# A hybrid decoder step: states, convolution rows, norm weights and sub keys laid out with channels or state dimension on the partitions

## The chip, the cores and the metric

One core of a Trainium2 chip. The metric is the time of one execution in device microseconds, as the median of several runs. All data are float32.

## What is computed

One step of a two-layer decoder trunk for 256 prompt tokens and 64 sample tokens (8 sequences of 8). Layer 0 is a Mamba-2 mixer, a PEER mixer and a per-layer embedding; layer 1 is dilated attention over a shared K/V, a PEER mixer and an embedding. The change touches the Mamba mixer of layer 0 and PEER's sub keys:

```python
def mamba_mixer(u, conv_buf, h0, w_in, conv_w, conv_b, dt_bias, a_log, d_skip, norm_g, w_out):
    zxbcdt = u @ w_in                                   # z 2048, xBC 4096, dt 32 columns
    xbc, new_buf = causal_conv(xbc, conv_buf, conv_w, conv_b)   # 4 taps, the last 3 rows are kept
    xbc = silu(xbc)                                     # xs 2048 (32 heads of 64), B and C 8 groups of 128
    dt = softplus(dt + dt_bias); a = -exp(a_log)
    y, h = ssd_scan(xs, dt, a, bm, cm, h0)
    y = (y + d_skip * xs) * silu(z)
    y = group_rmsnorm(y) * norm_g                       # 8 groups of 256
    return y @ w_out, new_buf, h
# in ssd_scan, per chunk and group of 4 heads (state h: 64 x 128 per head)
    y = ((C B^T) * decay) @ (xs dt) + (C h) * exp(cum)
    h = h * exp(cum[-1]) + B^T (tail * xs dt)
# in peer: scores of the queries against sub_keys (2 x 128 keys of 128)
```

The prompt starts from zero states; each sample sequence starts from its own state and convolution rows. New convolution rows and final states are outputs. Each PEER mixer picks 128 experts a token, gathers 4 KB rows of two tables for them, and sums.

## The kernel before

The program is written engine by engine, with explicit semaphores; TensorE writes into 8 PSUM banks used in turn (`claim` waits until the bank's last user is done, `freeing` marks that). Up to the first gather it goes through these stages:

1. `norm`, `dt`, then z (`gate_block`, L598): four blocks of 512 columns over all 320 tokens. Between the first and the second block PE transposes the 29 convolution rows (24 state rows, 4 taps, 1 bias) and the norm's weights (L625 to L629); ACT copies them to `stT` and `ngT` (L1467).
2. The xBC projection (L641), 32 channel blocks with channels on the partitions, each with POOL's copies of state rows (L2543 to L2546), ACT's eviction, DVE's convolution and silu; `to_tokens` turns the results back. Then PE turns the new convolution rows (L652), ACT copies them (L1500), SP stores them in 16 pieces (L1279, L1280).
3. `cum` and `ec`: cumulated decays, and the whole decay of each sample sequence and head (L804 to L813).
4. The scan: 24 steps, 8 groups for each of two prompt tiles of 128 tokens and for the sample tile (t = 2). In a step PE makes the decay and C B^T products of the next step (`scan_front`), then y and the state update (`scan_back`); DVE masks, adds and gates; POOL scales by dt and decays (L2550 to L2589); ACT takes exponentials and squares. The prompt's final states are turned by PE (`final_state`, L700), copied by ACT (L1568) and stored per group.
5. In a sample step two blocks of state (two heads, 8 sequences) are in turn: SP loads a block as (head, channel) x sequence x state dimension (L1295), PE turns 16 pieces of 128x128 (`sample_turn`, L657), ACT copies them to `h0T` (L1558), PE reads the states with C (L675) and makes the update (L683), POOL scales the unturned state (L2589), DVE adds the update into `hnew` (L2138), SP stores it (L1286). Beside these steps run the prompt tile's output products (`out_block`, L779), PEER's queries (L762) and scores (L747), and from group 3 on DVE's picks of experts (L2063 and on).
6. POOL starts the gathers (L2610) when the scan is over (L2202), the last states are stored and the first experts are chosen. From there a written order of phases interleaves gathers, dot products on DVE (L2255), sums on PE (L1129) and the rest of the network; SP streams the weights.

SP issues all other transfers in one fixed order and waits in that order; weights go through a ring of four 1 MB slots.

## Time and profile before

| | |
|---|---|
| median of 3 runs | 2504.68 us (2501.03 to 2508.19) |
| the profiled execution | 2497.27 us |
| its span, first to last instruction | 2495.5 us |
| PE busy | 1745.5 us (70%) |
| DVE busy | 1569.1 us (63%) |
| POOL busy | 1339.7 us (54%) |
| ACT busy | 305.7 us (12%) |
| read from HBM, written | 845.26 MB, 12.17 MB |

The span is the time inside the core; the execution's own time has about 2 us around it. PE's busy time is of pipelined products and says little of how near its peak it is; the shares are means over stages that have different limits. The profile attributes idle time of an engine to what ended it; of an engine that isn't the limit of its stage it costs nothing.

### The profile page before, as it was taken

The page shows a single profiled execution, that of the slowest core. Times are in us where ns is not written, and L with a number is a line of the kernel's source. Part 1 is how long each engine was busy: PE and PEld are TensorE (multiplying, and loading weights), DVE is VectorE, ACT ScalarE, POOL GpSimd, SP SyncE. Part 2 cuts the span into 40 slices and gives each one's busy share as a digit, 9 for nine tenths or more (in the row PEclk, how much of TensorE's full clock was granted, in tenths as well). Part 3 has the DMA queues.
Part 4 walks back from the last instruction along what each step waited for, and adds up shares of the span by engine and source line. Part 5 has one row for each costly group of instructions (what it writes and reads, how often), then busy time and mean ns, then how long its engine had stood idle before and what let it go on. Part 6 is the DMA issues. An engine that isn't in the chain of part 4 may idle for free.

```text
span 2495.5 us, 23767 instructions
## 1 busy us (share of the span) xinstructions
PE 1745.5 (70%) x7752; PEld 786.5 (32%) x7752; DVE 1569.1 (63%) x3811; ACT 305.7 (12%) x709; POOL 1339.7 (54%) x1496
## 2 busy tenths in 40 slices
PE   7999789594406666678787767776745758556678
PEld 4577758433400010022334224341213422001112
DVE  2488767999798657652635989768754543833321
ACT  2133313101000000001101012110012200000000
POOL 0011634266547777755674456655454643577774
PEclk9999899796756677789799787887878969699999
DMA  4331256499979999999999999999999989999997
GB/s 158 129 108 68 94 173 231 136 398 416 417 265 413 420 420 420 420 411 416 400 418 416 416 416 372 418 415 415 415 385 365 349 318 365 388 419 420 419 419 308
DMA packets 325848, 859.14 MB, mean 344 GB/s; under 512 B 26841, under 2 KB 93353, under 8 KB 325697
## 3 DMA queue, kind: packets, MB, share of 16 engines
q0 software_dynamic: 184320, 671.17, 66.5%
q1 hardware_dynamic: 141406, 186.46, 20.9%
q8 instruction: 62, 1.02, 0.2%
q14 instruction: 60, 0.49, 0.1%
HBM read 845.26 MB, written 12.17 MB: 344 GB/s over the span
## 4 chain that ended last, share of the span: by engine, by line
POOL 21%; DMA 17%; PE 12%; issue 9%; DVE 8%; SPq 4%; ACT 0%; POOLq 0%; DVEq 0%; ACTq 0%
POOL arena L2610 21%; DMA arena<-peer_v,arena 7%; PE banks L922 4%; DMA wring<-w_q 4%; PE banks L1129 3%; DVE arena L2255 3%; DMA wring<-cache_v 2%; SPq L1365 2%; PE banks L1038 1%; SPq L1363 1%; DMA wring<-peer_w_query 1%; DMA wring<-w_kv 1%; PE banks L860 1%; PE banks L565 1%; DMA arena<-peer_u,arena 1%
## 5 line engine op out<-in xcount | busy, mean ns | idle before, releaser
L2255 DVE SCALAR_TENSOR_TENSOR arena<-arena,banks 128x1024 f32<-128x1024 f32 x640 | 762.0, 1219 | 408.0 <-DMA arena<-peer_u,arena 401.9
L1129 PE MATMUL banks<-arena 128*32 128x512 f32 x2560 | 678.8, 714 | 334.8 <-DMA arena<-peer_v,arena 328.3
L2610 POOL DMA_INDIRECT arena<-peer_v,arena x640 | 608.3, 951 | 401.1 <-issue 202.2
L2610 POOL DMA_INDIRECT arena<-peer_u,arena x640 | 605.3, 946 | 380.6 <-issue 189.7
L1129 PEld LDWEIGHTS banks<-arena 128*32 128x32 f32 x2560 | 91.1, 116 | 795.8 <-DMA arena<-peer_v,arena 630.6
L922 PE MATMUL banks<-wring,uT 128*128 128x512 f32 (+3 forms) x448 | 223.3, 648 | 59.6 <-DMA wring<-w_q 26.5
L565 PE MATMUL banks<-cst,arena 128*128 128x128 f32 (+6 forms) x498 | 75.6, 299 | 161.5 <-DVE arena L2271 82.5
L922 PEld LDWEIGHTS banks<-wring,uT 128*128 128x128 f32 (+1 forms) x448 | 80.1, 189 | 209.1 <-issue 164.7
L646 PE MATMUL banks<-uT,wring 128*128 128x320 f32 x512 | 139.1, 433 | 0.0
L565 PEld LDWEIGHTS banks<-cst,arena 128*128 128x128 f32 (+6 forms) x498 | 58.9, 153 | 212.1 <-DVE arena L2271 82.7
L646 PEld LDWEIGHTS banks<-uT,wring 128*128 128x128 f32 x512 | 96.7, 190 | 39.8 <-issue 0.4
L2545 POOL COPY arena<-arena 128x3 f32<-128x3 f32 x32 | 6.0, 187 | 176.2 <-ACT arena L1491 176.2
L565 PE MATMUL banks<-cst,u 128*128 128x128 f32 (+1 forms) x256 | 43.3, 332 | 74.0 <-DVE u L1936 62.9
L860 PE MATMUL banks<-uT,wring 128*128 128x128 f32 x512 | 69.5, 294 | 9.6 <-issue 9.6
L860 PEld LDWEIGHTS banks<-uT,wring 128*128 128x128 f32 x512 | 64.2, 205 | 34.0 <-issue 34.0
L609 PE MATMUL banks<-wring,uT 128*128 128x512 f32 (+1 forms) x256 | 73.2, 499 | 0.0
L2063 DVE MAX8 arena<-arena 128x8 f32<-128x128 f32 (+1 forms) x208 | 60.6, 333 | 19.1 <-ACT arena L1528 18.2
L2066 DVE FIND_INDEX8 arena<-arena 128x8 uint32<-128x128 f32 (+1 forms) x208 | 67.3, 336 | 0.0
L565 PEld LDWEIGHTS banks<-cst,u 128*128 128x128 f32 (+1 forms) x256 | 35.6, 180 | 99.8 <-DVE u L1936 58.7
L1157 PE MATMUL banks<-wring,uT 128*64 128x512 f32 (+1 forms) x128 | 59.1, 614 | 3.4 <-DVE uT L2038 3.4
L2306 DVE TENSOR_SCALAR arena<-arena 128x512 f32<-128x512 f32 (+1 forms) x10 | 4.4, 441 | 86.8 <-ACT arena L1666 86.6
L1038 PE MATMUL banks<-wring,arena 128*64 128x128 f32 x208 | 28.0, 299 | 41.6 <-DMA wring<-cache_v 40.2
(271 smaller groups left out, 1971.9 us busy)
## 6 DMA issues: line engine op xcount, KB each, us to landing
wring<-peer_w_query SPq DMA_DIRECT2D x40, 1024.0 KB, 18.6
wring<-ssm_w_in SPq DMA_DIRECT2D x24, 1024.0 KB, 7.3
wring<-w_q SPq DMA_DIRECT2D x18, 1024.0 KB, 22.7
wring<-ssm_w_out SPq DMA_DIRECT2D x16, 1024.0 KB, 8.6
wring<-ple_w_gate SPq DMA_DIRECT2D x12, 1024.0 KB, 11.8
arena<-peer_u,arena POOLq DMA_INDIRECT x640, 10.0
arena<-peer_v,arena POOLq DMA_INDIRECT x640, 8.9
out_sample_ssm<-arena SPq DMA_DIRECT2D x16, 512.0 KB, 5.6
```

What stands on the lines that cost most here:

```text
L565: mm = pe.transpose(bank[0:c, col:col + r], src, ident[0:r, 0:r])
L609: mm = pe.matmul(out, uT[:, kk, OFF[t]:OFF[t] + ROWS[t]], cols, start=(kk == 0), stop=(kk == KD - 1))
L646: mm = pe.matmul(acc[:, 0:NTOK], w[k // 4][:, k % 4, j * 128:(j + 1) * 128], uT[:, k, :], start=(k == 0), stop=(k == KD - 1))
L860: mm = pe.matmul(bank[:, 0:R], w[k // 4][:, k % 4, (b % 4) * 128:(b % 4 + 1) * 128], uT[:, k, OFF[t]:OFF[t] + R], start=(k == 0), stop=(k ...
L922: mm = pe.matmul(bank[0:ROWS[t], 0:w.shape[2]], uT[:, kk, OFF[t]:OFF[t] + ROWS[t]], w[:, k, :], start=(kk == 0), stop=(kk == kchunks - 1))
L1038: pe.matmul(bank[rows, 0:128], pts[:, b, rows], cache[:, 1, 13 * b2 + b, :], start=(b == 0), stop=False)
L1129: mm = pe.matmul(sums(t, at, half), place_of(t, at), rows_buf[:, k, half * 512:(half + 1) * 512], start=at < spots(t), stop=False, skip_gr ...
L1157: mm = pe.matmul(acc[t][0:ROWS[t], :], uT[:, kk, OFF[t]:OFF[t] + ROWS[t]], w[:, k, :], start=(kk == 0), stop=(kk == 15))
L2063: step(j, dve.max(out_v[:, o], values))
L2066: step(j, dve.max_index(out_i[:, o], out_v[:, o], values))
L2255: dve.scalar_tensor_tensor(rows_buf[:, k, :], rows_buf[:, k, :], 1.0, u_now, ALU.mult, ALU.mult, accum_out=pact[:, n % 2, at:at + 1]).then ...
L2610: pool.indirect_dma_start(rows_buf[:, k, :], None, tables[kind], bass.IndirectOffsetOnAxis(ap=rows, axis=0))\
```

## The change

Inputs and outputs are laid out on the host so that the state dimension or the channels come first: convolution rows (128 x 32 x 29), the norm's weights (128 x 16), sub keys (128 x 2 x 128 a layer), sample states (8 groups x 128 x 8 sequences x 256), prompt states (128 x 8 x 256), new convolution rows (128 x 32 x 27). On the chip the transposes and copies that made these layouts go. A block of sample state is now one group of four heads for four sequences. POOL scales it out of its load buffer into `hnew` and so waits for that buffer's last store; DVE adds the update in place; the update has the sequence's B rows as weights and its x rows moving. The decay of each sequence and head comes from one product with a block-masked `da` that DVE writes. DVE waits for the store of the new convolution rows before it clears the scan's area.

```diff
-            pe.wait_ge(rows_in.sem, 64)
-            for half in range(2):
-                transposes(("rows", half), [(j * 29, conv_rows[:, (16 * half + j) * 128:(16 * half + j + 1) * 128])
-                                            for j in range(16)])
-            transposes("ng", [(0, ng_rows)])
...
-            for q in range(8):
-                for j in range(4):
-                    pe.wait_ge(*pool_done.at(("newrow", 4 * q + j)))
-                transposes(("newst", q), [(j * 128, newT[:, 4 * q + j, :]) for j in range(4)])
...
-                for i in range(2):
-                    for q in range(2):
-                        pe.wait_ge(*freed(("h0T", 2 * g + i, q)))
+                for q in range(2):
+                    pe.wait_ge(*h0_in[(2 * g + q) % 4].at(2 * g + q))
                 bank = claim(pe, ("inter", 2, g))
                 for b in range(8):
                     for i in range(2):
-                        mm = pe.matmul(bank[64 * i:64 * i + 64, 0:128], ctm[:, g % 2, b, :], h0T[:, i, b, :],
+                        mm = pe.matmul(bank[64 * i:64 * i + 64, 0:128], ctm[:, g % 2, b, :],
+                                       h0[(2 * g + b // 4) % 4][:, b % 4, 128 * i:128 * i + 128],
                                        start=(b == 0), stop=(b == 7))
...
+                acc = {(q, c): claim(pe, ("hupd", 2 * g + q, c)) for q in range(2) for c in range(2)}
+                for b in range(2):
                     for q in range(2):
-                        rows = slice(64 * i + 32 * q, 64 * i + 32 * q + 32)
-                        bank = claim(pe, ("hupd", 2 * g + i, q))
-                        mm = pe.matmul(bank[:, :], xdtt[rows, x, i * 128:(i + 1) * 128],
-                                       bm[rows, g % 2, :, :], start=True, stop=True)
-                        mm.then_inc(*full(("hupd", 2 * g + i, q)))
+                        for c in range(2):
+                            rows = slice(64 * c + 32 * q, 64 * c + 32 * q + 32)
+                            mm = pe.matmul(acc[q, c][:, 256 * b:256 * b + 256], bm[rows, g % 2, 2 * c + b, :], xdtt[rows, x, :],
+                                           start=True, stop=True)
...
             bank = claim(pe, "ec")
-            for hd in range(HEADS):
-                rows, k = slice(64 * (hd % 2), 64 * (hd % 2) + 64), hd // 2
-                mm = pe.matmul(bank[rows, k * 8:(k + 1) * 8], da[0:64, 2, hd:hd + 1].to_broadcast([64, 64]),
-                               cst[0:64, C_BM:C_BM + 8], start=True, stop=True)
-            mm.then_inc(*full("ec"))
+            pe.matmul(bank[:, 0:256], ones[0:64, :], da_of, start=True, stop=True).then_inc(*full("ec"))
...
+            sp.wait_ge(*pool_done.at(("newrow", CONV_BLKS - 1)))
+            sp.dma_start(O["new_conv"], newT).then_inc(*newst_out.mark("all", 16))
...
                 if blk >= 4:
-                    sp.wait_ge(*dve_done.at(("hnew", blk - 4)))
...
+                    sp.wait_ge(*pool_done.at(("h0s", blk - 4)))
+                    sp.wait_ge(*full_at(("inter", 2, blk // 2 - 2)))
...
-            for g in range(6):
-                store_final(g)
+            store_final(0)
             sp.wait_ge(*full_at(("state", 1, 7)))
             load_state(2)
             load_state(3)
+            store_final(1)
             load_weights(sp, load_index[("out", 0, 0)] + 8)
-            for g in (6, 7):
-                store_final(g)
...
                 if t == 0:
-                    sp.dma_start(sk_raw, I["peer_sub_keys"][1].rearrange("c k d -> k c d")).then_inc(*sk_in.mark(1, 16))
+                    sp.wait_ge(*full_at(("score", 0, 2, 1)))
+                    sp.dma_start(skT, I["keys_T"][1]).then_inc(*sk_in.mark(1, 16))
...
-            for q in range(8):
-                dve.wait_ge(*full_at(("newst", q)))
+            dve.wait_ge(*newst_out.at("all"))
             s(dve.memset(ctm[:, :, :, :], 0.0), dve_done, "scan_area")
+            s(dve.tensor_tensor(da_of.rearrange("p (g b h) -> p g b h", g=GROUPS, b=8),
...
-                    if blk >= 2:
-                        dve.wait_ge(*hnew_out[blk % 2].at(blk - 2))
-                    for q in range(2):
-                        bank = filled(dve, ("hupd", blk, q))
-                        freeing(dve.tensor_tensor(hnew[:, i, 4 * q:4 * q + 4, :], h0[blk % 4][:, 4 * q:4 * q + 4, :],
-                                                  bank.rearrange("p (b n) -> p b n", b=4), ALU.add), ("hupd", blk, q))
+                    for c in range(2):
+                        bank, rows = filled(dve, ("hupd", blk, c)), hnew[:, q, 2 * c:2 * c + 2, :]
+                        freeing(dve.tensor_tensor(rows, rows, bank.rearrange("p (b n) -> p b n", b=2), ALU.add), ("hupd", blk, c))
...
-                        s(pool.tensor_tensor(hh, hh, spread(ec[:, blk, :], 128), ALU.mult), pool_done, ("h0s", blk))
+                    for q in range(2):
+                        blk = 2 * g + q
+                        pool.wait_ge(*h0_in[blk % 4].at(blk))
+                        if blk < 2:
+                            pool.wait_ge(*hfin_out.at(1))
+                        else:
+                            pool.wait_ge(*hnew_out[q].at(blk - 2))
+                        s(pool.tensor_tensor(hnew[:, q, :, :].rearrange("p b (h c) -> p (b h) c", c=64),
+                                             h0[blk % 4].rearrange("p b (h c) -> p (b h) c", c=64),
+                                             spread(ec[:, blk, :], 64), ALU.mult), pool_done, ("h0s", blk))
```

On PE one sample step (group 2), before: turned states, decay, C B^T, y, the read with C, the update, then queries and scores.

```order
L565 MATMUL banks<-cst,u 128x128 x16
L694 MATMUL banks<-cst,arena 64x64 x4
L697 MATMUL banks<-arena 64x64
L717 MATMUL banks<-arena 64x64 x4
L675 MATMUL banks<-arena 64x128 x16
L683 MATMUL banks<-arena 128x512 x4
L762 MATMUL banks<-uT,wring 128x128 x32
L747 MATMUL banks<-arena 128x128 x4
```

And the same step with the change (line numbers are those of the changed kernel):

```order
L673 MATMUL banks<-cst,arena 64x64 x4
L676 MATMUL banks<-arena 64x64
L691 MATMUL banks<-arena 64x64 x4
L651 MATMUL banks<-u,arena 64x128 x16
L661 MATMUL banks<-arena 128x256 x8
L730 MATMUL banks<-uT,wring 128x128 x32
L715 MATMUL banks<-arena 128x128 x4
```

The 16 transposes at the head are gone; the read takes the loaded states themselves; the update is eight products of 256 columns where it was four of 512.

On POOL the scaling of the states in group 1 and the step behind it, before, with the semaphores that each instruction waits for (`bank_full`: PE's results; `vector_result`: DVE's):

```order
L2589 TENSOR_TENSOR arena<-arena,small 128x1024 [waits bank_full7,bank_full0,bank_free5,pool_result]
L2589 TENSOR_TENSOR arena<-arena,small 128x1024 [waits bank_full2,bank_full1,pool_result]
L2572 TENSOR_TENSOR arena<-arena,small 128x256 [waits bank_full2,bank_full7,bank_free1,vector_result,bank_free4,pool_result]
L2573 TENSOR_TENSOR arena<-arena,small 128x256 [waits pool_step]
L2575 TENSOR_TENSOR arena<-arena,small 128x256 [waits pool_result]
```

And with the change:

```order
L2509 TENSOR_TENSOR arena<-arena,small 128x1024 [waits state_loaded2,state_stored0,bank_free2,pool_result]
L2509 TENSOR_TENSOR arena<-arena,small 128x1024 [waits state_stored1,state_loaded3,pool_result]
L2490 TENSOR_TENSOR arena<-arena,small 128x256 [waits bank_full4,bank_full1,bank_free6,vector_result,bank_free1,pool_result]
L2491 TENSOR_TENSOR arena<-arena,small 128x256 [waits pool_step]
L2493 TENSOR_TENSOR arena<-arena,small 128x256 [waits pool_result]
```

The scaling waited for PE's transposes and now waits for the block's load and for the store of the block two before; what follows on POOL is the same.

On SP the transfers from the convolution's end to the second group of sample states, before:

```order
L273 DMA wring<-ssm_w_out 128x4x512 x4
L1295 DMA u<-state_ssm 128x8x128 x2
L1301 DMA out_prompt_ssm<-arena 128x2x128 x6
L1295 DMA arena<-state_ssm 128x8x128 x2
L273 DMA wring<-ssm_w_out 128x4x512 x4
L1301 DMA out_prompt_ssm<-arena 128x2x128 x2
L1295 DMA u<-state_ssm 128x8x128
L1286 DMA out_sample_ssm<-arena 128x8x128
```

And with the change:

```order
L1235 DMA out_new_conv<-arena 128x864
L273 DMA wring<-ssm_w_out 128x4x512 x4
L1250 DMA u<-state_T 128x1024 x2
L1255 DMA out_prompt_ssm<-arena 128x1024
L1250 DMA arena<-state_T 128x1024 x2
L1255 DMA out_prompt_ssm<-arena 128x1024
L273 DMA wring<-ssm_w_out 128x4x512 x4
L1250 DMA u<-state_T 128x1024
L1240 DMA out_sample_ssm<-arena 128x1024
```

Sixteen stores of convolution rows ahead of this piece have become its first row, and the last prompt states are stored ahead of the second four weights, not behind them.

## Rows read from the trace of the kernel before

**Rows 1.** Stages of core 0: length; busy PE, PEld, DVE, ACT, POOL; clock, DMA share, GB/s.

```profile
106.00:254.00 148.00, 145.36 (x607) 105.46 (x605) 124.96 (x321) 50.86 (x124) 19.65 (x95) 1.00 0.26 92
254.00:262.00 8.00, 8.00 (x92) 7.78 (x92) 0.21 (x1) 3.91 (x10) 4.12 (x6) 0.52 0.58 156
...
300.00:331.00 31.00, 26.84 (x182) 23.85 (x181) 28.70 (x61) 9.52 (x27) 19.17 (x23) 0.91 0.09 26
...
420.00:498.00 78.00, 49.90 (x428) 42.44 (x427) 73.72 (x238) 16.98 (x39) 23.96 (x21) 0.77 0.51 162
...
1000.00:2495.00 1495.00, 1034.67 (x4438) 384.89 (x4436) 834.29 (x2008) 155.14 (x345) 884.71 (x932) 0.85 0.99 396
```

**Rows 2.** Timeline of POOL: start, duration, instruction, idle before and its releaser.

```profile
346.49 3.87 POOL L2589 TENSOR_TENSOR u<-u,small 128x1024 f32<-128x1024 f32 x2 [12.95 <-PE banks L565]
...
497.90 1.14 POOL L2610 DMA_INDIRECT arena<-peer_u,arena  x1 [24.41 <-issue]
```

**Rows 3.** Timeline of all engines, the first z block's end.

```profile
45.38 2.22 PE L565 MATMUL banks<-cst,arena 29*128 29x29 f32 x33
```

**Rows 4.** Timeline of PE, convolution's end to the first decay product.

```profile
253.27 0.38 PE L804 MATMUL banks<-small,cst 128*128 128x32 f32 x2 [2.64 <-DVE arena L1993]
...
256.06 3.58 PE L811 MATMUL banks<-cst,small 64*64 64x8 f32 x64
259.57 2.07 PE L694 MATMUL banks<-cst,arena 128*128 128x128 f32 x8
```

**Rows 5.** Timeline of POOL, the same stretch.

```profile
248.24 0.20 POOL L2546 COPY arena<-arena 128x24 f32<-128x24 f32 x1
254.35 2.15 POOL L2554 TENSOR_TENSOR arena<-cst,small 128x512 f32<-128x512 f32 x2 [5.91 <-issue]
```

**Rows 6.** Timeline of PE, end of the prompt part and sample groups 0 to 3.

```profile
329.71 0.65 PE L724 MATMUL banks<-arena 128*128 128x256 f32 x2
...
331.55 13.90 PE L779 MATMUL banks<-wring,uT 128*128 128x512 f32 x32
345.28 1.91 PE L565 MATMUL banks<-cst,u 128*128 128x128 f32 x16
...
352.53 3.68 PE L675 MATMUL banks<-arena 128*64 128x128 f32 x32 [3.87 <-DVE h L2045]
...
360.71 14.00 PE L779 MATMUL banks<-wring,uT 128*128 128x512 f32 x32 [0.41 <-DVE arena L2138]
...
394.60 1.91 PE L565 MATMUL banks<-cst,u 128*128 128x128 f32 x16
...
398.44 1.97 PE L675 MATMUL banks<-arena 128*64 128x128 f32 x32 [0.47 <-ACT arena L1558]
400.34 1.14 PE L683 MATMUL banks<-arena 32*128 32x512 f32 x8
...
409.55 1.91 PE L565 MATMUL banks<-cst,arena 128*128 128x128 f32 x16
```

**Rows 7.** Timeline of DVE, sample groups 0 to 3.

```profile
374.82 0.69 DVE L2045 TENSOR_TENSOR h<-h,banks 128x512 f32<-128x512 f32 x1 [10.35 <-PE banks L779]
...
377.80 1.84 DVE L1923 TENSOR_TENSOR small<-small 128x1 f32<-128x1 f32 x1
...
412.43 0.22 DVE L2019 TENSOR_TENSOR arena<-banks,cst 64x64 f32<-64x64 f32 x1 [5.40 <-PE banks L697]
413.98 0.93 DVE L2022 TENSOR_TENSOR arena<-arena 64x256 f32<-64x256 f32 x1 [1.33 <-ACT arena L1515]
...
418.31 1.41 DVE L2138 TENSOR_TENSOR arena<-arena,banks 128x512 f32<-128x512 f32 x2
...
421.57 0.49 DVE L2063 MAX8 arena<-arena 128x8 f32<-128x128 f32 x2
...
481.44 1.41 DVE L2138 TENSOR_TENSOR arena<-arena,banks 128x512 f32<-128x512 f32 x2
```

**Rows 8.** Stores of the sample states, time from issue to landing.

```profile
DMA to landing us min/median/max: 2.9/5.6/7.1
```

151 lines of the change are left out of this document (48 added, 103 removed).

## The prediction, made before the changed kernel ran

> **What bounds the kernel now.** I read the stages first [rows 1]. From about 498 us to the end the DMA engines are busy 99% of the time: the experts' rows stream in at 396 GB/s, and nothing the change touches lies there. That stretch has no due date of its own: every wait in it is on work of the same stretch. So it starts when the first gather starts, and the question is only how much earlier that is. The first gather of POOL stands at 497.90, after the scan has been declared over [rows 2]. Everything the change alters at a price lies ahead of it, in three places with three different limits:
>
> - Up to about 250 us PE is the limit: in 106 to 254 it works 145.36 of 148 us at full clock, and the z product before it likewise follows PE. A PE instruction taken out there moves everything behind it.
> - In 254 to 262 a chain of small things runs from the last convolution block to the first decay matrix, with PE at a granted clock of 0.52.
> - In the sample third of the scan (331 to 498) PE is the limit until about 418, and DVE from then on: in 420 to 498 it works 73.72 of 78 us in 238 instructions [rows 1], which with the small gaps between so many is all of it. In the prompt part (300 to 331) DVE has 28.70 of 31, so there PE's and ACT's savings buy nothing.
>
> **The change, part by part.**
>
> *Convolution rows and the norm's weights loaded already turned.* 33 transposes leave PE between the first and second z block: 2.22 us [rows 3]. PE waits for no load there, and the rows' load is of the same size as before and still ahead of the same weights in SP's queue. **-2.2.** The three ACT copies that go were beside PE's work: nothing. The two waits on the load that DVE and POOL get come 60 us after its issue: nothing.
>
> *The new convolution rows stored from where they lie.* 32 transposes on PE, eight ACT copies and 16 stores go, one store comes. PE then waits for the last convolution block anyway (253.27, idle 2.64 for DVE [rows 4]), so the transposes were covered. The new cost: DVE may declare the scan's area free only when that store has landed, and POOL's first decay matrix is queued behind that. The store is issued after POOL's last row copy, 248.4 [rows 5]; no store like it is in the trace, the nearest are the sample states' stores of 512 KB (this is 432 KB), which take 2.9 to 7.1 us, 5.6 in the middle [rows 8]: landed at 251.3 to 255.5, I take 254.0. Between DVE's end and POOL's first decay lie 1.1 us (253.27 to 254.35), so that is at 255.1, done 1.1 later (two take 2.15 [rows 5]), at 256.2.
>
> *The sample decays of each sequence in one product.* 64 records of 3.58 us (at 256.06 [rows 4]) become one product of 256 columns. Bounds for it: nothing below, and above twice the pair for 128 columns, 2.07/4 = 0.52 at that clock (259.57 [rows 4]), so 1.0; I take 0.7. Its operand is one more DVE product right behind the clearing, at about 255.5, so PE doesn't wait. The first decay product then starts at 256.06 + 0.7 = 256.8 in place of 259.57: **-2.7**, -1.8 with the slowest landing, -3.5 as the most.
>
> *Final prompt states stored as they lie.* Two transposes and an ACT copy per group go, behind a DVE that is full: nothing in the prompt part. Two places count. The first output product (13.9 us) need not wait for a last pair of them: it starts behind the state product, 330.4, not 331.55 [rows 6]: -1.2. And the store of the last half is queued on SP ahead of weights that are needed 15 us later, so it lands near 342, before POOL needs it.
>
> *Sample states with the state dimension on the partitions.* Per group 16 transposes go from PE, four copies from ACT, and PE's wait for these copies. The read product and the update keep their columns (16 x 128; 4 x 512 become 8 x 256, taken at 1.14 us (400.34 [rows 6]), at most twice that if the eight loads of weights set the pace). POOL's scaling keeps its 1024 elements, about 1.95 us each (3.87 for two [rows 2]). Walked through:
>
> - Group 0. Between the end of the first output product (345.4) and the second (360.71) PE spent 15.3 us: transposes 1.84, small products, an idle 3.87 for DVE, and a read product at the low clock, 3.68 instead of 1.97 [rows 6]. Now the first output product ends at 344.3, and 0.9 of small products later DVE makes its mask (345.2). From mask to state additions DVE takes 5.88 us in group 3 (412.43 to 418.31 [rows 7]), 1.33 of it waiting for ACT's copies, which are gone; with one addition to h more (0.69 [rows 7]) it adds at 350.4. It has freed y's bank a microsecond earlier, which the last turned rows take, and the addition frees the bank for the second output product. With the transposes between them (1.9) that starts at 351.5: **-9.2** with the 1.2.
> - Group 1. DVE waits for that product (374.82, idle 10.35); the norm behind it lost time to POOL's scaling beside it (one 128x1 product took 1.84 [rows 7]), about 2.8 in all. POOL's scaling of this group now falls into DVE's wait, so that goes: **-12.0** at the first queries.
> - Groups 2 and 3: PE's own round, 394.60 to 409.55 [rows 6], loses 1.84 of transposes and 0.47 of wait: 14.95 becomes 12.6. Twice: **-16.6**. In group 3 DVE's decay product also waited 1.33 for ACT (413.98 [rows 7]), which was copying turned states: some 0.7 of it goes. DVE's picks start at 404.3, not 421.57: **-17.3**.
> - From there DVE is full, and its instructions are the same ones in the same order. So -17.3 stays, and PE, which gets its banks from DVE, follows.
>
> *Sub keys* go the same way: two transposes and a copy each, off the path; the second load now waits for the last scores of layer 0, long computed when SP comes to it. Nothing.
>
> **Sum:** -2.2 - 2.7 - 17.3 = **-22.2 us**; the first gather at about 476. The profiled execution took 2497.3 (span 2495.5), so it becomes 2475.1; the median of the runs shown is 7.4 above that execution, so on that scale 2504.7 - 22.2 = **2482.5**.
>
> **The rivals.**
>
> *Slower: the store-and-scale circle.* Before, DVE's addition waited for the store of two blocks ago. Now POOL scales into that buffer, so POOL waits for the store, and POOL's next `xdt` and `ctm`, which PE needs, are queued behind. The circle: addition 1.41 [rows 7], signal, one load and the store issued (about 1), landing, POOL 1.95, next block's addition: landing + 4.5. With 5.6 that is 10. The rounds I worked out give it 26, 12.6 and 12.8 us, and the four in the full DVE stretch 15.8 on average (418.31 to 481.44 [rows 7]), so it fits. Landing at 10 would cost 4 in all; from 14 on (18.5 a round: 5.9 + 5.7 + 4 x 2.7 = 22) the gain is gone, and at 16 it is 7.9 + 7.7 + 4 x 4.7 = 34 against 22: **2517**. For it: stores share their queues with 1 MB weight loads. Against it: the longest landing is 7.1 [rows 8], and runs of 4 KB take the place of runs of 512 bytes. Chance 0.04.
>
> *Low clock.* Where PE had waited 3.87 us, its next products ran at 1.2 GHz (3.68 against 1.97 [rows 6]), and in 254 to 262 it had 0.52. The transposes that go were also what kept PE working; if groups 1 to 4 start cold, each loses about 2.3, and the chain at 254 another 1: the gain is **-12**, 2492.7; chance 0.10. Against it: in groups 2 to 4 the waits between the products go too, and seven microseconds of queries stand in each. The Trainium skill, "TensorE: Matmul & The Clock Gate" (Part 1: The HAM clock gate), says that the throttled clock is the default and that activity releases it, which speaks for this rival. The rows bear it out where PE idles, and not inside a dense round.
>
> *More collisions, or fewer, of POOL and DVE.* POOL's scaling falls into another part of DVE's round; a hit costs DVE up to one scaling (1.9). In the full DVE stretch there are ten scalings: the gain goes to -14 (2490.7, chance 0.12) or to -28 (2476.7, chance 0.08).
>
> *The gain is swallowed:* the gathers start earlier and the end stays, 2505. For it only that the last four fifths are the same DMA stream; against it, that the stream is 99% full and so can't stretch without a new wait. Or the change moves no critical wait at all. Chance 0.08.
>
> **How the numbers follow.** Forecast -18 to -26: 0.58. Smaller gain by clock or collisions, -8 to -18: 0.10 + 0.12. Larger, -26 to -32: 0.08. No change: 0.08. Slower: 0.04. A difference of 0.3% (7.5 us) is about what can be told from none here; the first three cases are beyond it: faster 0.88, same 0.08, slower 0.04. The range takes the forecast, the larger gain and most of the smaller: 2474 to 2494.
>
> **What would show it.** Right: first gather at 474 to 479, and the same 1997.6 us from it to the end of the span; first decay product near 254.6 (with the 2.2); second output product near 347; PE's rounds of groups 2 and 3 near 12.6; DVE without idle from about 400; POOL's scalings released by stores and done before DVE's additions. Wrong: DVE idle ahead of its additions with POOL or a store as releaser (the circle); read products above 3 us in groups 2 to 4 (clock); a first gather near 476 with an end that hasn't moved (swallowed).

## The result, and the profile after

The changed kernel takes **2481.64 us** (median of 4 runs, 2479.28 to 2484.34), the kernel before 2502.86 (4 runs, 2499.72 to 2508.19): a ratio of **0.9913**, 95% interval 0.9892 to 0.9935. 2482.5 was predicted. The profiled execution took 2481.1 (span 2479.3). So the total came out right; the terms that make it up did not all do so, and the profile shows which.

Stages of the changed kernel (columns as in [rows 1]):

```profile
106.00:254.00 148.00, 142.19 (x572) 102.05 (x570) 124.06 (x320) 48.96 (x120) 20.37 (x95) 0.99 0.29 103
254.00:262.00 8.00, 7.67 (x37) 6.92 (x38) 1.65 (x4) 1.74 (x5) 4.73 (x6) 0.50 1.05 406
300.00:331.00 31.00, 26.61 (x166) 22.56 (x164) 28.41 (x61) 7.53 (x21) 19.66 (x24) 0.89 0.04 18
410.00:487.00 77.00, 37.25 (x369) 32.45 (x369) 72.82 (x234) 6.86 (x21) 23.47 (x20) 0.74 0.42 152
1000.00:2479.00 1479.00, 1031.51 (x4420) 385.63 (x4418) 824.63 (x1985) 154.78 (x344) 877.22 (x923) 0.85 1.00 397
```

The last four fifths are still one DMA stream, DVE is still full ahead of it. New is that PE stands idle for 6.13 us before 254, where it was 2.64, and that its granted clock is low in two more places, the end of the prompt part and the first queries (0.50 is 1.2 GHz, 1.00 is 2.4). First the changed kernel there, then the kernel before in the same two places of its program:

```profile
326.00:335.00 9.00, 7.95 (x27) 5.70 (x28) 8.35 (x20) 1.78 (x7) 5.21 (x7) 0.62 0.18 62
374.00:383.00 9.00, 6.90 (x40) 6.37 (x39) 6.65 (x16) 1.47 (x3) 0.78 (x1) 0.62 0.33 112
```

```profile
326.00:335.00 9.00, 7.39 (x37) 4.32 (x36) 8.35 (x20) 2.76 (x8) 5.40 (x7) 1.00 0.44 123
385.00:394.00 9.00, 7.54 (x67) 7.33 (x67) 5.99 (x13) 2.03 (x5) 0.00 (x0) 1.00 0.34 99
```

Timeline of PE in the changed kernel (start, duration, instruction, idle before and its releaser):

```profile
254.33 0.60 PE L771 MATMUL banks<-small,cst 128*128 128x32 f32 x2 [6.13 <-DVE arena L1912]
...
258.02 1.20 PE L777 MATMUL banks<-arena,cst 64*128 64x256 f32 x2
259.14 2.07 PE L673 MATMUL banks<-cst,arena 128*128 128x128 f32 x8
...
327.05 1.11 PE L673 MATMUL banks<-cst,arena 64*64 64x64 f32 x8 [1.61 <-DVE arena L1926]
...
332.07 14.77 PE L747 MATMUL banks<-wring,uT 128*128 128x512 f32 x32
...
353.09 14.00 PE L747 MATMUL banks<-wring,uT 128*128 128x512 f32 x32
...
373.68 1.40 PE L560 MATMUL banks<-cst,u 128*128 128x128 f32 x8 [2.15 <-issue]
...
377.15 9.51 PE L730 MATMUL banks<-uT,wring 128*128 128x128 f32 x64 [2.07 <-DVE arena L2102]
386.59 0.68 PE L673 MATMUL banks<-cst,arena 64*64 64x64 f32 x8
...
399.26 0.67 PE L673 MATMUL banks<-cst,arena 64*64 64x64 f32 x8
```

These answer to [rows 4, 6]. The sums behind the convolution take 0.60 a pair where they took 0.38. The first output product starts at 332.07 and not at 330.4, the second at 353.09 (before 360.71), the first queries at 377.15 (before 387.38) but take 9.51 in place of 7.38. The rounds of groups 2 and 3 are 12.67 (386.59 to 399.26), as worked out.

Timelines of DVE and of POOL in the changed kernel:

```profile
403.49 1.86 DVE L2100 TENSOR_TENSOR arena<-arena 64x256 f32<-64x256 f32 x1
...
407.91 1.41 DVE L2058 TENSOR_TENSOR arena<-arena,banks 128x512 f32<-128x512 f32 x2
...
409.54 0.49 DVE L1985 MAX8 arena<-arena 128x8 f32<-128x128 f32 x2
```

```profile
403.17 1.90 POOL L2509 TENSOR_TENSOR arena<-arena,small 128x1024 f32<-128x1024 f32 x1 [3.08 <-DMA out_sample_ssm<-arena]
...
487.14 1.15 POOL L2530 DMA_INDIRECT arena<-peer_u,arena  x1 [21.16 <-issue]
```

DVE's picks came at 409.54 (404.3 predicted, 421.57 before), the first gather at 487.14 (476 predicted, 497.90 before [rows 2]).

Because the start of the program scatters (below), the milestones of all profiled executions stand here behind the first sum product, which follows the last convolution block. All are read from the timelines; the last column is from the first gather to the end of the span.

| us | convolution's products start | sums start | first decay product | output 1 | output 2 | queries(0) (length) | picks | first gather | gather to end |
|---|---|---|---|---|---|---|---|---|---|
| before | 101.18 | 253.27 | +6.30 | +78.28 | +107.44 | +134.11 (7.38) | +168.30 | +244.63 | 1997.6 |
| before, second execution | 100.95 | 253.04 | +6.81 | +78.78 | +107.78 | +134.43 (7.38) | +168.62 | +245.28 | 1999.2 |
| after | 102.24 | 254.33 | +4.81 | +77.74 | +98.76 | +122.82 (9.51) | +155.21 | +232.81 | 1992.2 |
| PE busy from the start | 99.43 | 251.52 | +4.82 | +75.86 | +97.54 | +121.50 (9.75) | +153.05 | +230.02 | 1997.4 |
| large fillers in the scan | 99.61 | 251.73 | +4.82 | +77.32 | +97.65 | +125.05 (7.31) | +154.15 | +231.46 | 1995.0 |
| scaling cut out | 100.14 | 252.23 | +4.82 | +77.71 | +98.75 | +122.80 (9.52) | +153.76 | +224.29 | 1996.4 |
| two parts undone | 103.76 | 255.86 | +3.40 | +75.01 | +96.19 | +120.14 (9.49) | +151.42 | +229.39 | 1996.1 |
| filler ahead of the sums | 98.44 | 250.53 | +2.63 | +76.38 | +97.26 | +121.31 (9.44) | +153.87 | +233.13 | 1996.6 |
| small fillers in the scan | 100.22 | 252.33 | +4.82 | +75.41 | +95.71 | +122.73 (7.66) | +152.18 | +229.42 | 1998.3 |
| scaling on ACT | 102.64 | 254.73 | +4.82 | +77.73 | +98.63 | +122.69 (9.45) | +153.99 | +233.48 | 1996.8 |
| both fillers, scaling on ACT | 102.18 | 254.27 | +2.63 | +72.56 | +92.87 | +120.17 (7.39) | +149.37 | +229.23 | 1998.4 |
| scaling on ACT, decay first | 100.38 | 252.47 | +4.82 | +75.94 | +97.58 | +121.54 (9.71) | +154.03 | +226.18 | 1994.3 |
| the same with both fillers | 102.96 | 255.06 | +2.63 | +72.56 | +92.87 | +120.12 (7.45) | +149.36 | +219.93 | 1993.4 |
| one part undone | 102.03 | 254.12 | +4.15 | +76.53 | +98.03 | +122.08 (9.74) | +153.62 | +231.80 | 2006.5 |

Up to the picks, five of these executions run the changed kernel's code behind the sums: after, PE busy from the start, scaling cut out (which leaves out POOL's scaling alone), and the two with scaling on ACT without fillers (which differ from group 4 on). Their picks lie between +153.05 and +155.21, and the changed kernel's own execution is the latest of them. A shift of 2 us at the picks against that one execution therefore shows nothing by itself.

### The profile page after: what moved, and what is told of

The parts are those of the page before. It is cut to its first block, busy times and chain, and to the rows that moved or that the text cites. A ratio compares the mean times of both kernels' runs of the same rounds, so it can differ in the third digit from the quotient of the medians.

```text
span 2479.3 us, 23168 instructions
## 1 busy us (share of the span) xinstructions
PE 1728.9 (70%) x7541; PEld 770.1 (31%) x7541; DVE 1568.0 (63%) x3812; ACT 276.9 (11%) x656; POOL 1341.7 (54%) x1496
## 4 chain that ended last, share of the span: by engine, by line
POOL 21%; DMA 19%; PE 11%; issue 8%; DVE 8%; SPq 4%; ACT 0%; POOLq 0%; DVEq 0%; ACTq 0%
POOL arena L2530 21%; DMA arena<-peer_v,arena 8%; DMA wring<-w_q 4%; PE banks L882 4%; DVE arena L2174 3%; PE banks L1089 2%; SPq L1317 2%; DMA wring<-cache_v 2%; DMA wring<-w_kv 1%; SPq L1315 1%; PE banks L998 1%; DMA arena<-peer_u,arena 1%; DMA wring<-peer_w_query 1%; PE banks L822 1%; PE banks L560 1%
## 5 line engine op out<-in xcount | busy, mean ns | idle before, releaser
L882 PE MATMUL banks<-wring,uT 128*128 128x512 f32 (+3 forms) x448 | 217.8, 634 | 60.1 <-DMA wring<-w_q 28.2
L560 PE MATMUL banks<-cst,arena 128*128 128x128 f32 (+2 forms) x349 | 58.0, 317 | 161.4 <-DVE arena L2190 82.0
L560 PEld LDWEIGHTS banks<-cst,arena 128*128 128x128 f32 (+2 forms) x349 | 44.8, 163 | 205.3 <-DVE arena L2190 82.2
L560 PE MATMUL banks<-cst,u 128*128 128x128 f32 (+1 forms) x192 | 34.8, 346 | 66.5 <-DVE u L1855 59.7
L560 PEld LDWEIGHTS banks<-cst,u 128*128 128x128 f32 (+1 forms) x192 | 27.7, 190 | 91.5 <-DVE u L1855 55.7
```

The costliest lines, as they stand in the source:

```text
L560: mm = pe.transpose(bank[0:c, col:col + r], src, ident[0:r, 0:r])
L882: mm = pe.matmul(bank[0:ROWS[t], 0:w.shape[2]], uT[:, kk, OFF[t]:OFF[t] + ROWS[t]], w[:, k, :], start=(kk == 0), stop=(kk == kchunks - 1))
```

## The experiments

**1. PE busy from the start.** POOL fills a tile, and PE works on it while it waits for the first norm. `warm(n)` stands for n matmuls of 128x512 into the bank that is claimed next; nothing reads their results:

```
+            pe.wait_ge(*pool_done.at("warm"))
+            warm(14, arena)
             pe.wait_ge(*cst_in.at("cst"))
             norm_transposes("mix0")
```

> The changed kernel with 14 matmuls of 128x512 on a constant tile put ahead of PE's first transposes, in the time in which PE waits for the first norm (2 to 13.8 us). My reading of the changed kernel's trace: the 2.2 us of transposes that left the z phase were eaten because PE ran its dt products and the first z block at half pace until 33 us (a 128x128 weight load takes 0.34 us there and 0.19 behind it), 14 us of it against 6.5 us in the kernel before. If PE's idle start is the cause, dt takes about 6 us in place of 8.9, the z phase starts near 24 and the convolution's end near 247 in place of 254.3: about 7 us off the time. Rival: the pace of dt and of the first z block is set by something else than PE's clock (landing of weights, banks); then these products start where they did, to within 1 us, and the time stays within 3 us of the changed kernel's. Third: the extra matmuls run at low clock to beyond 13.8 and cost what they overrun.

2482.2 us (2478.85 to 2484.68, 4 runs), ratio 0.992 (0.9902 to 0.9937): no gain. Stages of that run (columns as in [rows 1]):

```profile
17.00:20.00 3.00, 1.28 (x15) 1.01 (x13) 0.00 (x0) 2.57 (x6) 0.21 (x1) 1.00 0.51 187
20.00:23.00 3.00, 3.00 (x28) 3.00 (x28) 0.19 (x1) 0.23 (x1) 0.00 (x0) 1.00 0.97 381
23.00:26.00 3.00, 3.00 (x39) 2.90 (x38) 0.19 (x1) 0.00 (x0) 0.00 (x0) 0.50 0.75 291
26.00:30.00 4.00, 4.00 (x7) 1.82 (x6) 1.54 (x7) 1.85 (x3) 0.00 (x0) 0.52 0.08 32
```

My theory of the idle start falls: PE had been at work since 1.3 us, and the granted clock still fell to 0.50 in 23 to 30, from the middle of the dt products (64 of 32 columns) into the first z block. What sets the pace there stays open. The fillers ran to 15.9 and cost what they overran (dt at 19.98 for 19.24); dt took 6.12 and not 8.86, so z began at 26.03, 2 us earlier than in the changed kernel's profile, but no earlier than in other runs of that unaltered start (25.85 to 28.81).

**2. Large fillers in the scan.** `warm` as in run 1, where PE waits:

```
             def scan_front(t, g):
...
+                if t == 1 and g >= 2:
+                    warm(1)
+                if (t, g) == (2, 0):
+                    warm(3)
...
-                    norm_transposes("ffn0", (0,))
+                    warm(4)
+                    norm_turns("ffn0", (0,))
+                    warm(4)
+                    norm_taken("ffn0", (0,))
```

> The changed kernel with extra matmuls of 128x512 where PE waits: one per group in groups 2 to 7 of the scan's second prompt tile, three ahead of the first sample group, four before and four behind the turned rows of group 1. My theory for the 5.7 us that are missing in the sample part: after the transposes went, PE idles enough there that its clock falls at 326 and again at 373 us; the last prompt products took 5.8 us in place of 3.4, and queries(0) 9.51 in place of 7.38. Then here the first output product starts near 330, queries(0) take about 7.4, DVE's first pick starts 4 to 5 us earlier relative to the convolution's end (155.2 us behind it in the changed kernel), and so does the first gather. Rival: DVE's chain paces these places and the clock only fills waits; then picks and gather stay where they are within 1 us, whatever the clock.

2479.03 us (2472.06 to 2481.19, 4 runs), ratio 0.9898 (0.9877 to 0.992). Timeline of PE in that run:

```profile
323.65 2.74 PE L560 MATMUL banks<-cst 128*128 128x512 f32 x6
...
373.24 3.70 PE L560 MATMUL banks<-cst 128*128 128x512 f32 x8 [1.02 <-DVE arena L2116]
376.78 7.31 PE L741 MATMUL banks<-uT,wring 128*128 128x128 f32 x64
```

The clock held: queries(0) took 7.31, the output products 13.9 each. But a matmul of 512 columns is two records here, 0.9 us and not 0.45, so the fillers were twice as long as I had meant and delayed what they were to speed up; the picks come 1.1 earlier than in the changed kernel's execution and not 4 to 5, which is within the scatter of its code. The run shows that the clock can be held, not what holding it is worth; run 6 has smaller fillers.

**3. Scaling cut out**, to 64 of 1024 elements of each block; the other elements of the sample states are left out, the waits stay.

```
-                        s(pool.tensor_tensor(hnew[:, q, :, :].rearrange("p b (h c) -> p (b h) c", c=64),
-                                             h0[blk % 4].rearrange("p b (h c) -> p (b h) c", c=64),
-                                             spread(ec[:, blk, :], 64), ALU.mult), pool_done, ("h0s", blk))
+                        s(pool.tensor_tensor(hnew[:, q, 0, 0:64].unsqueeze(1), h0[blk % 4][:, 0, 0:64].unsqueeze(1),
+                                             spread(ec[:, blk, 0:1], 64), ALU.mult), pool_done, ("h0s", blk))
```

> The changed kernel with POOL's scaling of the loaded states cut to 64 of 1024 elements (the rest of the state is left unscaled; the waits stay). It prices the collisions of POOL's scaling with DVE, and the circle of store and scaling. From the trace of the changed kernel: between DVE's first pick (409.5) and the first gather (487.1), DVE instructions that lie beside a scaling are longer than their like by 1.58, 0.83, 1.58 and 1.37 us, and one on the path before by 1.44: if these are collisions, that stretch shrinks from 77.6 to about 72 us, and the first gather comes about 7 us earlier relative to the convolution's end. If the scalings only lie beside DVE's work without slowing it, the stretch stays at 77.6. If the circle were what paces the sample groups, groups 4 to 7 would shorten by much more, up to 1.9 each on top.

2473.65 us (2471.85 to 2474.74, 4 runs), ratio 0.9882 (0.9866 to 0.9899). From picks to gather it takes 70.53 in place of 77.60: 7.07, somewhat over the 5.6 expected. Groups of DVE's instructions by line, first two of the changed kernel between picks and gather, then one of this run (busy time, mean ns, idle before):

```profile
L2022 DVE TENSOR_TENSOR arena<-arena 128x512 f32<-128x512 f32 x4 | 5.9, 1483 | 0.1
...
L2019 DVE TENSOR_TENSOR arena<-arena,cst 128x512 f32<-128x512 f32 x4 | 4.1, 1033 | 0.1
```

```profile
L2022 DVE TENSOR_TENSOR arena<-arena 128x512 f32<-128x512 f32 x4 | 2.8, 691 | 0.1
```

So collisions of POOL's scaling with DVE cost 7 us of this stretch: DVE's lengthened instructions of the changed kernel, each against its length here, add up to 7.05. DVE has next to no idle time to give back (0.3), and beyond those 7 nothing shortened, so the circle of store and scaling isn't what paces groups 4 to 7. The timelines of the changed kernel show what a collision is, POOL first, then DVE:

```profile
427.55 2.14 POOL L2509 TENSOR_TENSOR arena<-arena,small 128x1024 f32<-128x1024 f32 x1 [8.02 <-DMA out_sample_ssm<-arena]
```

```profile
427.96 2.27 DVE L2022 TENSOR_TENSOR arena<-arena 128x512 f32<-128x512 f32 x1
```

The scaling ends at 429.69, the product 0.54 behind it. The other three 128x512 products that began inside a scaling (447.05, 461.44 and 464.46) end 0.55 behind its end. A product of this form takes 0.69 alone, so each had stood nearly still until the scaling was over: a hit costs about what is left of the scaling. The product that had begun ahead of the scaling (427.23) kept its 0.69, and that scaling took 2.14 in place of 1.90.

**4. Two parts undone**: the convolution rows and the norm's weights are loaded as rows again, and the new rows are turned by PE again.

```
+            for half in range(2):
+                transposes(("rows", half), [(j * 29, conv_rows[:, (16 * half + j) * 128:(16 * half + j + 1) * 128])
+                                            for j in range(16)])
+            transposes("ng", [(0, ng_rows)])
...
+            for q in range(8):
...
+                transposes(("newst", q), [(j * 128, newT[:, 4 * q + j, :]) for j in range(4)])
...
-            sp.dma_start(O["new_conv"], newT).then_inc(*newst_out.mark("all", 16))
```

> The changed kernel with two of its parts undone: convolution rows and the norm's weights are loaded as rows and turned by PE (33 transposes), and the new convolution rows are turned by PE and stored as rows, as in the kernel before. What is left is the states with the state dimension on the partitions, the one product for the decays and the sub keys. By the prediction's terms the sum falls by 2.2 for the rows; the other undone part was predicted to cost or bring under 1 (its transposes were covered): so about 2.2 to 3 us above the changed kernel and 19 below the kernel before, first gather 17 to 19 us ahead of the kernel before's. By the changed trace, in which the part before the scan gained nothing, it would come out within 1 us of the changed kernel. If the store as it lies had a cost that covers the gain of the rows, it comes out below the changed kernel.

2485.78 us (2483.07 to 2487.64, 4 runs), ratio 0.9936 (0.9919 to 0.9952): 4.1 above the changed kernel (2.2 to 3 expected), with intervals that overlap, and 16.5 below before. The states, the decays and the sub keys carry most of the gain. The 4.1 does not lie between the sums and the gather, which comes at +229.39, earlier than in both executions of the changed code (+232.81, +230.02). Timeline of PE:

```profile
255.86 0.38 PE L784 MATMUL banks<-small,cst 128*128 128x32 f32 x2 [2.64 <-DVE arena L1942]
...
259.26 2.07 PE L686 MATMUL banks<-cst,arena 128*128 128x128 f32 x8
```

With the 32 transposes ahead of them the first sums run 0.38 a pair (the new product behind them again takes 1.20), and the first decay product comes 3.40 behind the first sum, 2.9 less than before and 1.4 less than in the changed kernel.

**5. Filler ahead of the sums**, where PE now idles 6.13 us:

```
+            warm(6)
             for q in range(6):
                 for t in range(3):
                     pe.wait_ge(*freed(("tok", q, t)))
```

> The changed kernel with six matmuls of 128x512 on the constants (0.87 us each) behind the last convolution product, where PE then waits 6.1 us for the last convolution block; nothing else. Theory: the 32 transposes of the new convolution rows had kept PE at work there, and without them PE enters the chain of sums at 1.2 GHz; from the first sum product to the first decay product the changed kernel takes 4.81 us and the same chain with those transposes put back 3.40. So it falls to about 3.4 here, and DVE's picks come about 1.4 us earlier behind the convolution's end, or less where DVE's full prompt part swallows it. Rival: the 1.4 us has another cause (ACT, the DVE product of the decays), then the chain stays at 4.8.

Timeline of PE in that run:

```profile
244.23 5.31 PE L560 MATMUL banks<-cst 128*128 128x512 f32 x12
250.53 0.38 PE L779 MATMUL banks<-small,cst 128*128 128x32 f32 x2 [0.99 <-DVE arena L1920]
...
253.16 1.98 PE L680 MATMUL banks<-cst,arena 128*128 128x128 f32 x8
```

The chain fell to 2.63, further than the 3.4 expected, and the theory of its clock stands. The picks came at +153.87, within the scatter of the changed kernel's code, and from there to the gather this execution took 79.26, 1.7 more than the changed kernel, so that the gather gained nothing; the time is 2481.28 (2480.32 to 2483.02, 4 runs), ratio 0.9912 (0.9894 to 0.993).

**6. Small fillers in the scan**: as run 2, with warm(1) of 256 columns, warm(1), warm(2) and warm(2).

> The changed kernel with smaller fillers than in the run before: one matmul of 256 columns (0.45 us) per group in groups 2 to 7 of the second prompt tile, one of 512 ahead of the first sample group, two before and two behind the turned rows of group 1 (1.75 us each, in waits of 2.15 and 2.07 us). The larger fillers held the clock at full speed but took 3.7 us where the wait was 2.1, and 2.7 where it was 1.6. Theory: now the clock holds and nothing is delayed: the first output product starts about 76 us behind the convolution's end (77.7 in the changed kernel), queries(0) take 7.3, and the picks come at about 150.5 us behind the convolution's end in place of 155.2; the first gather 4 to 5 us earlier on the same scale, the time about 2477. Rival: the clock fills waits only, DVE's chain paces: less than 1.5 us.

Timeline of PE:

```profile
327.74 13.90 PE L758 MATMUL banks<-wring,uT 128*128 128x512 f32 x32
...
371.90 3.37 PE L560 MATMUL banks<-cst 128*128 128x512 f32 x4 [2.06 <-DVE arena L2116]
375.06 7.66 PE L741 MATMUL banks<-uT,wring 128*128 128x128 f32 x64
```

The first output product starts 75.41 behind the sums (2.3 earlier, as expected), and the second 3.05 earlier. By the end of the first queries 1.1 of it is lost: they start only 0.1 earlier than in the changed kernel and win back 1.85 by their length (7.66 for 9.51). PE waited there for a bank that DVE frees, and my filler took that bank, began when the queries could have begun, and ran at low clock (3.37 for what took 1.98 at 366.31). The picks come 3.0 earlier than in the changed kernel's execution and 0.9 earlier than in the earliest of its code, the gather 3.4 and 0.6; the theory had 4.7 at the picks. The time doesn't show it: 2482.44 (2481.36 to 2483.38, 4 runs), ratio 0.9917 (0.99 to 0.9935). A gain of 3 is below what these medians tell apart.

**7. Scaling on ACT**, for groups 4 to 7, where ACT is busy 1.4 to 2.6 us of 15:

```
+                if t == 2 and 3 <= g < 7:
+                    for blk in (2 * g + 2, 2 * g + 3):
+                        act.wait_ge(*h0_in[blk % 4].at(blk))
+                        act.wait_ge(*hnew_out[blk % 2].at(blk - 2))
+                        for c in range(16):
+                            cols = slice(64 * (c % 4), 64 * (c % 4) + 64)
+                            ins = act.activation(hnew[:, blk % 2, c // 4, cols], h0[blk % 4][:, c // 4, cols], ACT.Copy,
+                                                 scale=ec[:, blk, c:c + 1])
+                        s(ins, act_done, ("h0s", blk))
...
-                    for q in range(2):
+                    for q in range(2 if g < 4 else 0):
```

The last two lines are POOL's; SP's loads and DVE's additions of these groups wait for ACT in place of POOL.

> The changed kernel with the scaling of the loaded states of groups 4 to 7 moved from POOL to ACT, as 16 copies of 64 columns with a scale per sequence and head block (about 0.25 us each, 4 us per state half of 512 KB, in a stretch where ACT is busy 1.4 to 2.6 of 15 us). With the scaling cut out, the stretch from DVE's first pick to the first gather had shrunk from 77.6 to 70.5 us. If POOL's scaling slows DVE because the two run side by side, and ACT's does not, the stretch falls to about 72 here and the time to about 2476. If any engine's scaling slows DVE as much, it stays near 77. If ACT, waiting for the store, holds up what PE or DVE need next (copies of queries, the next decay matrix), DVE shows idle time with ACT as releaser, and the stretch grows beyond 77.6.

2487.8 us (2486.84 to 2490.38, 4 runs), ratio 0.9941 (0.9923 to 0.996): slower than the changed kernel, by the third case. What DVE waited for between picks and gather (total, times, longest):

```profile
DVE arena L1954 <- ACT arena L1456: 9.0, 3, 3.1
```

The collisions are gone, but ACT's decay matrix of the next group stands in its queue behind 7.9 us of scaling, and DVE waits for that. From picks to gather it takes 79.49.

**8. The fillers of runs 5 and 6 with run 7.**

> The changed kernel with the fillers of the chain, the smaller fillers of the scan and the scaling of groups 4 to 7 on ACT, all together. If the three act on different stretches, their gains add: about 1.4 + 4 + 5 us, the first gather at about 223 us behind the convolution's end in place of 232.8, and the time near 2471 to 2473. If DVE's full prompt part takes back what the chain gives, 1.4 less.

2481.18 us (2477.07 to 2483.88, 4 runs), ratio 0.9906 (0.9887 to 0.9925). What ACT did spoils the sum, as in run 7 (79.86 from picks to gather). What the fillers do stands in the table: picks at +149.37.

**9. Scaling on ACT, decay matrix first.**

```
-                if n + 1 < 3 * GROUPS:
+                if n + 1 < 3 * GROUPS and n <= 2 * GROUPS + 3:
                     decay_exp(n + 1)
...
+                if t == 2 and 3 <= g < 6:
+                    decay_exp(n + 2)
                 if t == 2 and 3 <= g < 7:
                     for blk in (2 * g + 2, 2 * g + 3):
```

> The run before that moved the scaling of groups 4 to 7 to ACT, with one difference: ACT makes the decay matrix of the group after the next before it scales, not behind it. In that run DVE's instructions were all at their bare length (the four 128x512 products of the picks 0.69 each in place of 1.48), but DVE stood idle 9.0 us in three waits for ACT's decay matrix, queued behind 7.9 us of scaling. Theory: without these waits the stretch from DVE's first pick to the first gather falls from 79.5 to about 70.5 us, as with the scaling cut out, and the time to about 2475. Rival: ACT's later copies of queries and scores, which still stand behind the scaling, take the wait's place; then DVE idles for these and the stretch stays above 74.

2475.69 us (2474.7 to 2480.36, 4 runs), ratio 0.99 (0.9875 to 0.9924), 6 below the changed kernel. Groups of DVE's instructions between picks and gather:

```profile
L2069 DVE TENSOR_TENSOR arena<-arena,banks 128x512 f32<-128x512 f32 x16 | 11.0, 687 | 2.1 <-ACT arena L1503 1.6
...
L2033 DVE TENSOR_TENSOR arena<-arena 128x512 f32<-128x512 f32 x4 | 2.8, 692 | 0.1
```

72.15 from picks to gather: 5.45 won, and 1.6 lost in one wait for a scaling that came late.

**10. The same with the fillers of runs 5 and 6.**

> The same with PE's fillers in the chain at the convolution's end, in the second prompt tile and in group 1 (the run that had all three, with the decay matrix ahead of ACT's scaling). If the gains add: picks at 149.4 us behind the convolution's end, as in that run, and 70.5 from there to the first gather: 220 against 232.8 in the changed kernel and 244.6 in the kernel before; the time about 2470, 12 below the changed kernel.

**2471.46 us** (2463.12 to 2477.68, 6 runs), ratio **0.9873** (0.9849 to 0.9896): 10 below the changed kernel, below both kernels. Gather 219.93 behind the sums (220 expected). Stage between picks and gather, then two lines of PE's timeline:

```profile
404.00:475.00 71.00, 39.75 (x387) 34.76 (x386) 66.75 (x237) 38.54 (x150) 5.00 (x11) 0.76 0.47 170
```

```profile
327.62 13.90 PE L758 MATMUL banks<-wring,uT 128*128 128x512 f32 x32
...
375.18 7.45 PE L741 MATMUL banks<-uT,wring 128*128 128x128 f32 x64
```

**11. The kernel before, once more.**

> The kernel before, unchanged, for a second profiled execution. The profile of before that the prediction rests on took 2497.3, while the median of its runs is 2502.2 to 2502.9; the profiles of the two kernels differ by 16.2 and the medians by 21.2. In seven executions with the changed kernel's start, PE's convolution products began between 98.4 and 102.6 us. If that scatter is also the kernel before's, its products start here at another time than 101.18, between 99 and 104, and what lies behind (first gather 244.6 behind the convolution's end, 1997.6 to the end) is the same to within 2 us. If the missing 5 us lie in the scan or behind the first gather, one of these two numbers is larger here.

2499.3 us, one run. Convolution's products at 100.95, gather 245.28 behind the sums, 1999.2 from there: each within 2 us of the first execution, and none shows the 5 us by which the medians of the two kernels differ more than their profiles (21.2 and 16.2). The two profiles of before thus agree, and both lie below the median of its runs (2501.6 of 11 in this comparison).

**12. One part undone**: only the 32 transposes of the new rows and their 16 stores are back.

> The changed kernel with one part undone: the new convolution rows are turned by PE (32 transposes behind the last convolution product), copied by ACT and stored as rows in 16 pieces, as in the kernel before. The prediction took these transposes for covered work whose removal neither costs nor brings anything on PE. Theory now: they kept PE at full clock into the chain behind the convolution; so from the first sum product to the first decay product it takes 3.4 us in place of 4.8, and, as in the run with two parts undone, the first gather comes about 229.4 us behind the convolution's end in place of 232.8: this part of the change by itself then cost up to 3 us, and the time is 2479 to 2482, no higher than the changed kernel's. Rival, from the medians (the run with two parts undone took 4.1 more than the changed kernel, of which the rows' transposes explain 2.2): the part brought about 2, and the time here is near 2484.

2482.58 us (2471.65 to 2494.24, 6 runs), ratio 0.9914 (0.9891 to 0.9936). The chain took 4.15, between the two numbers: its first three pairs of sums ran 0.38, then the clock fell. The gather came 1.0 earlier than in the changed kernel's execution and not 3.4, and later than in the first experiment's. The profiled execution is the slowest of the six, by what lies behind the gather (2006.5). Runs this far apart tell neither theory from the other; that the new rows' transposes brought up to 1.4 us as cover for the clock is shown in the chain, that they pay as a whole is not.

## Why the prediction was right, and where it was not

**The result's signs.** The forecast had named the first gather at 474 to 479 and 1997.6 from it to the end as signs that it is right. The gather came at 487.14, 11 later than the 476 of the sum, and 1992.2 remained. So the time was met, and the account of where it comes from was not. The steps one by one:

**The bound.** DMA stream from the first gather, DVE full ahead of it, PE ahead of that: this held, and the gain was made where it was looked for. Behind the sums the first gather moved from +244.6 and +245.3 to +232.8 in the changed kernel's own execution, and to +230.0 in the first experiment's, whose code is the same from the sums on.

**Rows and norm loaded turned, -2.2.** Nearly right in size, hidden by scatter. From the first z product to the convolution's first, the kernels with the 33 transposes take 75.24 and 74.68 where dt took 6.4 to 6.9, and those without 72.59 to 74.21 where it took 6.8 to 7.8; where dt took 8.86, 75.79 with and 73.96 to 74.21 without: some 1.6 either way. The start itself scatters by more: with the same start the convolution began at 98.44 to 102.96, in ten executions. The changed kernel's profile had one of the slow starts, and its sums began 1.06 after before's.

**New rows' store and one product for the decays, -2.7.** The path was right: the store landed 3 us after its issue, DVE didn't wait for it, and PE didn't wait for DVE's product. Mis-sized were the terms on PE. The transposes that I called covered had been PE's last work, and without them the sums and the new product ran at 1.2 GHz. The forecast left the sums at their 2.79 and took "I take 0.7" for the product; from start to start they took 3.69 and 1.12, the latter above the bound of 1.0. The product's own record is 1.20 in place of the 0.68 at full clock (run 5), and the chain took 4.81, where the two executions with the transposes back took 3.40 and 4.15 (there too the clock falls within the chain, only later). -1.5 came, or -2.0 against before's second execution; -3.7 with a filler.

**Sample part, -17.3.** At the picks, chain included, -13.1 came of -20.0 (168.30 to 155.21 behind the sums; on that scale 148.3 was due). The steps that failed are "it starts behind the state product, 330.4" and the queries of group 1, which were left at 7.38, both for one reason: they took full clock for granted. The last prompt products and the first output product ran at low clock after 1.61 of idle (14.77), and queries(0) after two waits of 2.15 and 2.07 (9.51). The changed kernel's execution is 3.4 behind what was due at the first output product (1.2 of it from the chain), and 3.5 more come between the start of the first queries and the picks. Between these two places the walk through group 0 and the norm held: from the first output product to the first queries it took 45.08, where 55.83 less 10.8 was due. The second output product thus came 8.7 earlier behind the sums, where 9.2 and 2.7 were due, and 14.6 with the fillers.

In executions of the same code up to there the picks came at +153.05 to +155.21, so 4.8 to 6.9 were missing; with fillers in the chain and in the scan they came at +149.37 and +149.36, within 1.1 of what was due. So 3.7 of the missing part, and more in the changed kernel's own execution, is the clock, by experiment. It isn't a mere return of what was due: up to the first output product the fillers brought 1.8 more than that, and ahead of the queries they cost 3.4. And 1.1 in the changed kernel's own execution is no clock: the product at 403.49 lay beside the scaling at 403.17 and took 1.86, where it takes 0.77 in run 1 and in those with the fillers. The norm without POOL beside it (0.16 a product) and the rounds of groups 2 and 3 (12.6, measured 12.67 and 12.68) hold.

**The rival of the low clock** (-10 of the gain, chance 0.10) was the case that came, at a smaller price (5 to 6) and not where it was looked for: the read products stayed at 1.97 in groups 0 to 3, as "the waits between the products go too" had it, while idle places ahead of the chain, of the first output product and of the queries got colder. The Trainium skill, "TensorE: Matmul & The Clock Gate" (Part 1: The HAM clock gate), has the throttled clock as the default that activity releases; here the granted 0.50 of the stretch 254 to 262 bears it out, and keeping PE at work ahead of it gave 0.38 a pair again. The fall at 23 us in run 1, in the middle of PE's work, is not of that form.

**"So -17.3 stays."** Not quite: 77.60 in place of 76.33 from picks to gather. The instructions are the same, the collisions with POOL fell on other ones. The rival of more collisions had that form, priced at 8; 1.3 came. That the scaling costs 7 us there makes little difference between the kernels: against their lengths in run 3, the kernel before's instructions of this stretch are 5.8 too long in all, the changed kernel's 7.05, and 1.3 is what lies between. One of before's groups, to be held against the 691 of run 3:

```profile
L2100 DVE TENSOR_TENSOR arena<-arena 128x512 f32<-128x512 f32 x4 | 4.6, 1158 | 0.1
```

**The circle** closes as predicted (POOL waited for stores):

```profile
POOL arena L2509 <- DMA out_sample_ssm<-arena: 75.0, 14, 16.4
```

but it has room: the tightest scaling ended at 405.07 (403.17 + 1.90), its addition began at 407.91, 2.8 later. Stores landed after 3.7 in the middle, not 5.6. That rival was rightly small.

**The total.** At the first gather the two profiles differ by 10.8, at the end by 16.2, and the medians by 21.2. From the gather to the end the changed kernel's profile took 1992.2, the other executions of the same code 1993.4 to 2006.5. So 5.4 of the 16.2 lie in a stretch in which the change takes out only the turning of layer 1's sub keys, and that scatters by more than that. What the steps explain is 11.8 to 15.3 behind the sums (before's two executions against the two of the changed code) and 1.6 ahead of them: 13 to 17 of the 21.2, whose interval (ratio 0.9892 to 0.9935) reaches from 16 to 27. That the forecast of 22 met the total is in part luck: two errors of some 5 us stood against each other, a clock that it took for granted, and a remainder that no run places. What before's other runs have above its two profiles, 2 to 6 us, stays open.

## What to carry to other kernels

Before you take covered work from PE, look at its granted clock behind the wait that the work had filled: here the longer wait cost the chain 0.7 to 1.4 us, where the covered transposes had cost nothing. A filler in a wait is cheap as long as it needs nothing that the wait is for, its bank included. Work that two engines do side by side can have a price that no idle row shows: compare the mean duration of one instruction form between stretches, and try a third engine that is idle, with what its queue holds behind the moved work checked first. A total that comes out right says little on terms of 2 us where start and tail scatter by 5: judge steps by distances between neighbouring milestones.

## What the runs showed of the hardware that was not expected

The clock fell to 0.50 at 23 us in the run in which PE had worked since 1.3 (idle 1.72 ahead of dt), in the middle of the 64 dt products, as it did in other runs without that work. And the record of the granted clock can miss such a stretch. Stage of the changed kernel's dt products, then PE's weight loads behind them:

```profile
19.00:25.00 6.00, 5.76 (x28) 5.79 (x28) 0.19 (x1) 0.23 (x1) 0.00 (x0) 1.00 0.82 319
```

```profile
32.46 0.34 PEld L604 LDWEIGHTS banks<-wring,uT 128*128 128x128 f32 x1 [0.52 <-issue]
...
33.81 0.19 PEld L604 LDWEIGHTS banks<-wring,uT 128*128 128x128 f32 x1 [0.24 <-issue]
```

The column shows 1.00 throughout, but the loads take 0.34 until 33.3 and 0.19 from then on, and 28 products lie in this stretch where the kernel before has 50. In run 1 the same load takes 0.34 where the column shows 0.52 (26 to 30):

```profile
28.75 0.34 PEld L611 LDWEIGHTS banks<-wring,uT 128*128 128x128 f32 x1 [0.52 <-issue]
```

So the pace of one form of instruction is the surer sign.

POOL's scaling held up DVE's instructions that read two operands from SBUF (128x512 products, 0.69 alone, took up to 2.27 in the changed kernel), and it held them until it was over. The additions from a PSUM bank (L2058, 0.69 each) and the one-operand searches beside it kept their length. Not every one-operand instruction did: in the kernel before, a cast that takes 0.20 elsewhere ended 0.05 behind the scaling that it lay beside (471.59 + 1.90). DVE, then POOL, in the kernel before:

```profile
473.08 0.46 DVE L2088 CAST arena<-arena 128x64 f32<-128x64 uint32 x1
```

```profile
471.59 1.90 POOL L2589 TENSOR_TENSOR arena<-arena,small 128x1024 f32<-128x1024 f32 x1 [2.98 <-PE banks L565]
```

The Trainium skill, "GPSIMD Engine Reference" (1. Specifications), says that POOL shares its SBUF interfaces with VectorE, with contention for VectorE's instructions in a 2-port perf mode or with two SBUF inputs; the trace agrees for the latter, 1.48 on average against 0.69, and no run here shows in which mode the cast ran. ACT's scaling beside the same DVE instructions left them at 0.69.
